# Third mixer's squares, head sums, roots and rotary exchange as fill pieces beside the second mixer's end, in a fused two-layer decode step

## The reference, cut to what matters

```python
def rope_partial(x, pos):
    ...
    x1, x2 = xr[..., :half], xr[..., half:]          # half = 8
    rot = jnp.concatenate([x1 * cos - x2 * sin, x2 * cos + x1 * sin], axis=-1)
    return jnp.concatenate([rot.astype(x.dtype), x[..., ROPE_DIM:]], axis=-1)

q_c = rope_partial(rmsnorm(q_c.reshape(B, L, H_C, D_C), lp['qn_c']), pos)
k_c = rope_partial(rmsnorm(k_c.reshape(B, L, H_C, D_C), lp['kn_c']), pos)
```

## Time and profile before

| what | value |
|---|---|
| three runs, median (lowest to highest) | 1285.93 us (1282.99 to 1288.49) |
| the profiled execution: its time, its span | 1283.79 us, 1281.9 us |
| TensorE busy (PE) | 1234.9 us, 96% of the span |
| VectorE, ScalarE, GpSimd busy | 599.8, 355.2, 134.7 us |
| mean granted TensorE clock | 0.989 of full |
| HBM | 114 GB/s over the span |
| chain that ended last | TensorE 86%, issue 4%, VectorE 4%, ScalarE 2% |

### The profile page before, as it was taken

The page is one execution under the profiler, slowest core; times in us unless marked ns, Lnnn a source line. Parts: engine busy times, 40 slices in busy tenths (PEclk is TensorE's granted clock), DMA queues, the critical chain, the costliest instruction groups (busy, mean ns, idle before and its releaser), DMA issues.

```text
span 1281.9 us, 23685 instructions
## 1 busy us (share of the span) xinstructions
PE 1234.9 (96%) x9382; PEld 920.9 (72%) x9382; DVE 599.8 (47%) x1281; ACT 355.2 (28%) x802; POOL 134.7 (11%) x204
## 2 busy tenths in 40 slices
...
GB/s 229 224 104 67 44 102 156 121 33 79 93 28 62 160 261 168 117 166 162 67 114 182 106 66 58 158 117 116 35 66 102 19 83 177 252 173 67 213 99 37
DMA packets 143368, 150.15 MB, mean 117 GB/s; under 512 B 15736, under 2 KB 130462, under 8 KB 143132
## 3 DMA queue, kind: packets, MB, share of 16 engines
...
HBM read 135.19 MB, written 11.07 MB: 114 GB/s over the span
## 4 chain that ended last, share of the span: by engine, by line
PE 86%; issue 4%; DVE 4%; ACT 2%; SPq 1%; DMA 1%; POOL 1%; ACTq 0%; DVEq 0%; POOLq 0%
PE psum L1092 57%; PE psum L1019 5%; PE psum L1253 3%; PE psum L1269 2%; PE psum L1391 1%; ACT arena L1685 1%; PE psum L1275 1%; PE psum L1134 1%; DVE arena L2192 1%; PE psum L1628 1%; PE psum L1446 1%; PE psum L1230 1%; PE psum L1458 1%; PE psum L1473 1%; PE psum L1577 1%
## 5 line engine op out<-in xcount | busy, mean ns | idle before, releaser
L1092 PE MATMUL psum<-x_b,ring 128*128 128x288 f32 x1296 | 343.1, 414 | 1.9 <-DMA ring<-in_w_in 1.1
L1092 PE MATMUL psum<-x_a,ring 128*128 128x288 f32 x1296 | 343.6, 415 | 0.5 <-DVE x_a L2145 0.4
L1092 PEld LDWEIGHTS psum<-x_b,ring 128*128 128x128 f32 x1296 | 239.9, 192 | 78.5 <-issue 17.2
L1092 PEld LDWEIGHTS psum<-x_a,ring 128*128 128x128 f32 x1296 | 240.4, 192 | 77.7 <-issue 17.0
L1685 ACT ACTIVATE arena<-psum 128x512 f32<-128x512 f32 (+9 forms) x206 | 96.9, 489 | 221.9 <-PE psum L1019 88.8
L1092 PE MATMUL psum<-z,ring 128*128 128x288 f32 x384 | 102.1, 412 | 0.0
L1092 PEld LDWEIGHTS psum<-z,ring 128*128 128x128 f32 x384 | 70.1, 190 | 20.9 <-issue 3.4
L1019 PE MATMUL psum<-consts,arena 128*128 128x128 f32 (+2 forms) x446 | 63.9, 278 | 7.6 <-DMA arena<-in_x_prompt 5.0
L1019 PEld LDWEIGHTS psum<-consts,arena 128*128 128x128 f32 (+2 forms) x446 | 50.7, 143 | 26.5 <-issue 9.8
L1092 PE MATMUL psum<-merged,ring 128*128 128x288 f32 x256 | 64.1, 414 | 3.5 <-issue 2.4
L1685 ACT ACTIVATE arena<-arena 128x256 f32<-128x256 f32 (+7 forms) x104 | 44.8, 464 | 65.8 <-DVE arena L2624 28.9
...
## 6 DMA issues: line engine op xcount, KB each, us to landing
...
```

What stands on the lines that cost most here:

```text
L1092: ins = mm(out[:, 0:NTOK], lhs, rhs(k), **flags)
```

## The change

The third mixer's preparation becomes six entries of `fillers()`: `c_sq` 0 and 1 (ScalarE's squares; with the first, GpSimd clears `CSW`; with the second, SyncE exchanges), `c_rms` 0 and 1 (head sums on TensorE into a bank of the projections, root on ScalarE) and `c_turn` 0 and 1 (VectorE's rotation). They stand between the branch projection `p_up` (0, 7) and the gate projection `p_g` (8), and wait for `b_scale` (1, 2) in place of the second mixer's end. Since `CSW` is cleared first, four transfers of 8 partitions with all 8 tiles of queries and keys replace the twelve. Their SBUF is now the arena's start. The cache's first two key pages are fetched before `b_s0` (1, 0), and clearing `CQX` moves to that place on GpSimd. `FILL` is laid out anew for the whole layer.

```diff
-PROJECTIONS = ("p_a", "p_z", "p_ba", "p_f", "p_c", "p_g", "p_up", "p_y", "p_pg", "p_ple")
+PROJECTIONS = ("p_a", "p_z", "p_ba", "p_f", "p_c", "p_g", "p_up", "p_y", "p_pg", "p_ple", "c_rms")
...
         add("b_norm6", g, 1)
+        if g == 1:
+            add("c_fetch_k", 0)
+            add("c_fetch_k", 1)
         add("b_s0", g, 0)
...
         add("b_sdec", g, 1)
-    add("c_rms", 0)
-    add("c_rms", 1)
-    for q in range(4):
-        if q < 2:
-            add("c_fetch_k", q)
-        add("c_fetch_v", q)
     add("c_rope", 0)
     add("c_rope", 1)
+    for q in range(4):
+        add("c_fetch_v", q)
     add("c_nat", 0)
...
         whole("p_up", 0, m)
+    for part in ("c_sq", "c_rms", "c_turn"):
+        for i in range(2):
+            out.append((part, i))
     for m in range(8):
...
-FILL = [0, 0, 32, 6, 0, 10, 17, 0, 19, 0, 4, 0, 6, 3, 6, 3, 18, 2, 14, 3, 0, 1, 14, 3, 0, 0, 0, 0, 0, 1, 1, 0, 0, 0,
-        0, 0, 0, 0, 0, 0, 0, 0, 0, 0, 0, 0, 1, 0, 1, 2, 3, 4, 2, 2, 2, 1, 1, 2, 5, 0, 4, 0, 0, 7, 3, 0, 0, 1, 1, 0, 1,
-        0, 0, 0, 3, 8, 5, 5, 0, 1, 7, 3, 0, 0, 12, 0, 0, 15, 0, 19, 5, 17, 8, 12, 5, 0, 0, 0, 2, 5, 0, 1, 0, 0, 2, 5,
-        0, 0, 0, 0, 0, 0, 0, 0, 0, 0, 1, 0, 0, 0, 0, 0, 0, 0, 0, 0, 0, 0, 0, 0, 0, 0, 2, 0, 2, 2, 0, 2, 0, 0, 0, 0, 9,
-        0, 0, 0, 0, 5, 0, 1, 0, 2, 0, 1, 0, 1, 1, 1, 2, 5, 3, 0, 5, 1, 1, 2, 0, 2, 1, 1, 2, 5, 3, 1, 4, 4, 1, 1, 1, 4,
-        0, 1, 0, 3, 0, 9, 0, 0, 0, 0, 0, 0, 0, 0, 0, 0, 0, 0, 0, 0, 0, 0, 0, 0, 0, 0, 0, 0, 0, 0, 0, 0, 2, 0, 4, 0, 1,
-        1, 0, 1, 0, 2, 6, 0, 0, 1, 0, 1, 0, 2, 2, 1, 0, 0, 1, 3, 2, 3, 7, 3, 0, 5, 1, 0, 6, 1, 1, 0, 4, 0, 7, 2, 2, 3,
-        6, 7, 2, 0, 7, 1, 1, 3, 1, 7, 3, 4, 4, 0, 0, 0, 21, 0, 0, 1, 3, 6, 2, 0, 0, 0, 1, 2, 5, 0, 0, 4, 1, 0, 1, 6,
-        3, 0, 4, 3, 3, 1, 2, 0, 1, 6, 4, 1, 3, 6, 3, 3]
+FILL = [0, 0, 24, 9, 8, 0, 24, 5, 12, 3, 1, 2, 5, 4, 11, 4, 11, 2, 15, 3, 1, 0, 14, 3, 0, 0, 0, 0, 0, 1, 0, 0, 0, 0,
+        0, 0, 0, 0, 1, 0, 0, 0, 0, 0, 0, 0, 2, 0, 1, 2, 2, 5, 0, 3, 0, 2, 0, 1, 5, 0, 7, 0, 3, 0, 3, 0, 1, 0, 1, 1, 0,
+        0, 0, 0, 1, 11, 2, 5, 0, 0, 0, 14, 0, 0, 14, 0, 1, 11, 0, 27, 5, 15, 7, 10, 0, 4, 2, 1, 0, 4, 0, 1, 4, 0, 0,
+        5, 0, 0, 0, 0, 0, 0, 0, 0, 0, 0, 0, 0, 0, 0, 0, 0, 0, 0, 1, 0, 0, 0, 0, 0, 0, 0, 2, 0, 3, 1, 1, 1, 0, 0, 0, 3,
+        6, 0, 1, 0, 0, 1, 3, 0, 0, 4, 0, 1, 0, 1, 1, 2, 1, 4, 3, 0, 5, 2, 2, 4, 0, 0, 0, 0, 3, 5, 4, 0, 3, 4, 1, 1, 1,
+        4, 1, 1, 0, 2, 0, 8, 0, 0, 0, 0, 0, 0, 0, 0, 0, 0, 0, 0, 0, 0, 0, 0, 0, 0, 0, 0, 0, 0, 0, 0, 0, 0, 2, 0, 2, 3,
+        1, 2, 0, 0, 0, 3, 5, 0, 1, 0, 0, 3, 0, 0, 2, 1, 0, 0, 1, 2, 2, 4, 1, 0, 4, 3, 0, 7, 1, 3, 3, 1, 1, 0, 4, 1,
+        32, 1, 3, 3, 4, 4, 0, 1, 3, 0, 2, 5, 5, 0, 0, 2, 20, 0, 1, 3, 1, 6, 2, 1, 0, 0, 2, 0, 3, 2, 0, 3, 2, 0, 0, 7,
+        3, 0, 3, 4, 3, 2, 2, 0, 0, 5, 5, 2, 3, 5, 5, 3]
...
-        CSQ = CKT[:, :, :, :].rearrange("p s a n -> p (s a n)")[:, 0:4 * NTOK].rearrange("p (a n) -> p a n", a=4)
-        CSW = CKT[:, :, :, :].rearrange("p s a n -> p (s a n)")[:, 4 * NTOK:12 * NTOK].rearrange("p (i a n) -> p i a n", i=2, a=4)
-        SQ = (CSQ, CVN[:, :, :].rearrange("p a n -> p (a n)")[:, 0:4 * NTOK].rearrange("p (a n) -> p a n", a=4))
+        SQ = arena[:, 0:8 * NTOK].rearrange("p (i a n) -> p i a n", i=2, a=4)
+        CSW = arena[:, 8 * NTOK:16 * NTOK].rearrange("p (i a n) -> p i a n", i=2, a=4)
+        CMX = part(3, 4)
+        top[0] = CQX_AT
+        CQX = part(4, NSEQ, 32)
-        CMX = part(3, 4)
-        CQX = part(4, NSEQ, 32)
+        top[0] = CKR_AT
...
+        swapped = [(h + to, h + 8 - to) for h in (0, 64) for to in (0, 8)]
...
                                           A["state_rwkv"][l, :, 4 * g + 2 * pr + hh].rearrange("s v k -> v s k")).then_inc(S.sem("rw_state_loaded"), 16)
-            def c_rms(l, i):
-                evicted(sp, "p_c", l, 4 * i + 3)
-                sp.wait_ge(S.sem("b_done"), S.count("b_done"))
-                sp.wait_ge(S.sem("b_snew"), S.count("b_snew"))
-                for to, of, n in turned:
-                    sp.dma_start(CSW[to:to + n, i, :, :], QC[of:of + n, 4 * i:4 * i + 4, :]).then_inc(S.sem(f"c_sw{i}"), 16)
+            def c_sq(l, i):
+                if i == 0:
+                    return
+                evicted(sp, "p_c", l, 7)
+                sp.wait_ge(S.sem("c_cleared"), S.count("c_cleared"))
+                for to, of in swapped:
+                    sp.dma_start(CSW[to:to + 8, :, :, :], QC[of:of + 8, 0:8, :].rearrange("p (i a) n -> p i a n", i=2)).then_inc(S.sem("c_swapped"), 16)
             def fetch(cache, l, s, dst, name):
...
                     sp.wait_ge(S.sem("b_done"), S.count("b_done"))
+                if s >= 2:
+                    sp.wait_ge(S.sem("past_k_t"), S.count("past_k_t"))
+                fetch(A["cache_k"], l, s, CKR[:, s % 2], f"past_k{s % 2}_loaded")
+            def c_fetch_v(l, s):
+                if s == 0:
                     sp.wait_ge(S.sem("b_snew"), S.count("b_snew"))
                     sp.wait_ge(S.sem("states_stored"), S.count("states_stored"))
-                if s >= 2:
-                    sp.wait_ge(S.sem("past_k_t"), S.count("past_k_t"))
-                fetch(A["cache_k"], l, s, CKR[:, s % 2], f"past_k{s % 2}_loaded")
-            def c_fetch_v(l, s):
                 if s >= 4:
...
             def c_rms(l, i):
-                pe.wait_ge(S.sem("squares"), S.count("squares"))
+                n = proj_no[S.at]
+                pe.wait_ge(S.sem("squares"), S.count("squares", pos[("c_sq", l, i)]))
+                pe.wait_ge(S.sem(freed()), S.count(freed(), proj_at[n - 3]))
+                for h in range(4):
+                    ins = mm(bank()[32 * h:32 * h + 32, 0:NTOK], C("sum_head"), SQ[:, i, h, :], start=True, stop=True)
+                ins.then_inc(S.sem("projected"), 1)
+            def c_rope(l, i):
                 pe.wait_ge(S.sem("b_snew"), S.count("b_snew"))
-                sum4(i, SQ[i], C("sum_head"))
-            def c_rope(l, i):
-                pe.wait_ge(S.sem("inv_roots"), S.count("inv_roots", pos[("c_rms", l, 1)]))
+                pe.wait_ge(S.sem("inv_roots"), S.count("inv_roots", pos[("c_rms", l, i)]))
                 pe.wait_ge(S.sem("c_rope"), S.count("c_rope", S.at - 1))
-                spread4(SQ[i][:, 0, :], C("spread_head"), 32)
+                spread4(SQ[:, i, 0, :], C("spread_head"), 32)
             def c_nat(l, i):
...
                 act.wait_ge(S.sem("out_roots"), S.count("out_roots"))
+            def c_sq(l, i):
+                evicted(act, "p_c", l, 4 * i + 3)
+                act.wait_ge(S.sem("b_scaled"), S.count("b_scaled", pos[("b_scale", l, 1, 2)]))
+                fn(SQ[:, i, :, :], QC[:, 4 * i:4 * i + 4, :], ACT.Square).then_inc(S.sem("squares"), 1)
+                act.wait_ge(S.sem("squares"), S.count("squares"))
             def c_rms(l, i):
-                evicted(act, "p_c", l, NC3 - 1)
-                act.wait_ge(S.sem("b_done"), S.count("b_done"))
-                act.wait_ge(S.sem("b_snew"), S.count("b_snew"))
-                fn(SQ[i][:, :, :], QC[:, 4 * i:4 * i + 4, :], ACT.Square).then_inc(S.sem("squares"), 1)
-                act.wait_ge(S.sem("squares"), S.count("squares"))
-                act.wait_ge(S.sem("square_sums"), S.count("square_sums"))
-                inv_root(SQ[i][:, 0, :], M[i][:, 0:NTOK], 1.0 / 64, "c_eps").then_inc(S.sem("inv_roots"), 1)
+                act.wait_ge(S.sem("projected"), S.count("projected"))
+                fn(SQ[:, i, 0, :], bank()[:, 0:NTOK], ACT.Ln, bias=C("c_eps"), scale=1.0 / 64).then_inc(S.sem(freed()), 1)
+                act.wait_ge(S.sem(freed()), S.count(freed()))
+                fn(SQ[:, i, 0, :], SQ[:, i, 0, :], ACT.Exp, scale=-0.5).then_inc(S.sem("inv_roots"), 1)
                 act.wait_ge(S.sem("inv_roots"), S.count("inv_roots"))
             def c_nat(l, i):
...
+                act.wait_ge(S.sem("states_stored"), S.count("states_stored"))
...
-            def c_rms(l, i):
-                dve.wait_ge(S.sem(f"c_sw{i}"), S.count(f"c_sw{i}"))
+            def c_turn(l, i):
+                dve.wait_ge(S.sem("c_swapped"), S.count("c_swapped"))
...
                           "states_stored")
-            def c_nat(l, i):
+            def c_sq(l, i):
                 if i == 0:
+                    pool.wait_ge(S.sem("b_scaled"), S.count("b_scaled", pos[("b_scale", l, 1, 2)]))
+                    pool.memset(CSW[:, :, :, :], 0.0).then_inc(S.sem("c_cleared"), 1)
+                    pool.wait_ge(S.sem("c_cleared"), S.count("c_cleared"))
+            def c_fetch_k(l, s):
+                if s == 0:
+                    pool.wait_ge(S.sem("b_done"), S.count("b_done"))
+                    link(pool.memset(CQX[:, :, :, :], 0.0))
+            def c_rope(l, i):
+                if i == 0:
                     pool.wait_ge(S.sem("c_rope"), S.count("c_rope"))
-                    pool.wait_ge(S.sem("b_snew"), S.count("b_snew"))
```

(29 more changed lines are left out.)

6 lines of the change are left out of this document (3 added, 3 removed).

## The result

The changed kernel takes 1276.82 us (median of 15 runs, 1273.32 to 1279.46) against 1282.99 us of the kernel before in the same session (15 runs, 1277.82 to 1291.55): ratio 0.9942, interval 0.9924 to 0.996. The forecast was 1275.3 us, 10.6 us less than 1285.93, within 1268 to 1287, and faster by more than 0.5%. The time lies in the range, 1.5 us over the forecast; it is faster by 0.58%, and the interval (0.40 to 0.76%) reaches under 0.5%. The measured gain, 6.2 us by the medians, is less than the 10.6. The profiled executions took 1283.79 and 1277.75 us.

A forecast was written before the change was run, and what follows sets the result against it. It took TensorE's work, its waits and its lower clock to bound the kernel. Terms +0.4 - 2.9 - 4.2 - 1.0 - 6.8 + 1.9 + 0.6 + 1.4 = -10.6 us off 1285.93 gave 1275.3 us, range 1268 to 1287.

The forecast's parts named there:

- The move itself: Third mixer's preparation in its new place: stays hidden but for a 0.2 us wait at `b_norm5`, +0.4 us for both layers.
- rival 2: At `b_norm5`: the exchange lands late, TensorE waits 3.8 us, with lower clock behind it; 1289.3 us, chance 0.09.
- `a_sout`: TensorE's wait ahead of `a_sout`: three more pieces cover 1.45 of 1.80 us, -2.9 us for two layers.
- `b_lora`: TensorE's wait of 2.09 us ahead of `b_lora`: five more pieces cover it, -4.2 us.
- `a_u`: TensorE's wait ahead of `a_u` (2): 11 pieces become 12, -0.5 of 0.75 us each, -1.0 us.
- `a_spread` and `a_convout`: Ahead of `a_spread` 0 and `a_convout`: one piece fewer at each, a payment of +1.9 us.
- `b_kk`: Between `b_lora` 0 and `b_kk`: 22 pieces become 20, a payment of 0 to +1.9 us, taken +0.6.
- `c_sout` (1) to `p_up` 2: Behind `c_sout` (1): 3 pieces become 1, so TensorE waits 0.7 us, a payment of +1.4 us.
- The clock: Half-clock stretches behind three long waits at `a_sout` and `b_lora` go, -6.8 us, bounds 0 and -6.8.
- Rival 1: TensorE's clock: the lower level comes at other places instead; sum -3.8, 1282.1 us, chance 0.18.
- Rival 3: Places pieces are taken from: waits of the same size come up there instead; 1286 us, chance 0.13.
- rival 4: The preparation's new place gives nothing and all gain is `FILL`'s; no time of its own, no chance given.

The follow-up runs named there:

- e9: The kernel before with the new `FILL` up to `a_norm5` (2) alone, its own behind it: 1281.7 us, ratio 0.9968.
- e3: The kernel before with four more pieces ahead of `b_lora` 0 alone, taken from between there and `b_scale` (0, 0): 1281.0 us, ratio 0.9982.
- e11: The kernel before with the next layer's parameter loads put behind the last `p_up` instead of ahead of it: 1281.4 us, ratio 0.9971.
- e2: The kernel before with the new `FILL` up to `b_scale` (0, 0), its own behind it, third mixer not moved: 1274.8 us, ratio 0.9944.
- e5: The changed kernel with pieces moved to places where it waits, as many as before ahead of `b_hist`: 1272.8 us, ratio 0.9894.
- e6: The kernel before with the new `FILL` up to `b_scale` (0, 0), pieces in it moved to where TensorE waited, third mixer not moved: 1272.0 us, ratio 0.9891.

## Why the prediction was right, and where it was off

**The move itself: sizes right, its end slightly over.** Memset 2.04 us (2.1 forecast), fourth issue from 434.98 (435.0), release at 438.94 (438.8), rotation over at 447.25 (447.2), `b_norm5`'s product at 447.70 (447.6), TensorE there at 447.37 (447.5). Differences of 0.1 us on both sides made 0.48 us out of 0.2: +1.0 in place of +0.4 us. The landing scattered by more than that, from 2.8 to 4.0 us after the end of the last issue over the fourteen times that the seven kernels with the new place made it. One argument against rival 2 was wrong: each of the four transfers has the 8 partitions of those that did the exchange before, with twice the tiles, and not an eighth of the partitions.

**`a_sout`: -2.1 in place of -2.9.** Three more pieces should have covered 1.45 of 1.80 us and covered 1.06. The chain did behave as forecast: from the start of `a_sout` 0 to the end of VectorE's last layout it took 10.71 us before (183.97 to 194.68) and 10.72 after (187.20 to 197.92). The term that was mis-sized is the price of a piece. Timeline before (the rest is in the earlier trace rows), then of the changed kernel:

```profile
183.97 1.13 PE L1340 MATMUL psum<-arena 32*128 32x512 f32 x4
...
185.02 0.75 PE L1092 MATMUL psum<-x_b,ring 128*128 128x288 f32 x2
```

```profile
187.20 1.99 PE L1349 MATMUL psum<-arena 32*128 32x512 f32 x8
...
189.12 7.06 PE L1101 MATMUL psum<-x_b,ring 128*128 128x288 f32 x28
...
194.94 2.98 DVE L2390 TENSOR_TENSOR arena<-arena,consts 64x512 f32<-64x512 f32 x1
```

The lone piece between `a_sout` 0 and 1 was taken away. With it TensorE needed 2.79 us up to the first piece behind `a_sout` 1 (183.97 to 186.76), without it 1.92: the piece had held 0.87 us, not 0.485. The four more pieces in the long row are 1.94; 1.94 - 0.87 = 1.07 us.

**`b_lora`: -3.5 in place of -4.2.** I had counted five pieces from `a_norm5` (2). The runs show four. The chain starts where ScalarE reads the last piece of a `p_z` tile (204.77 us before): from there to `b_lora` it takes 17.14 us before, 17.14 in e9, 17.13 in e3 and 17.31 in the changed kernel. That piece has a fixed place in the list, so what counts is how many pieces of the list stand ahead of `b_lora`, 279 before and 283 after. 4 x 0.485 = 1.94 of the 2.09 us; e9 and e3 bear it out, and in the changed kernel 0.32 us are left.

**`a_u`** gave 1.0 us as forecast. **`a_spread` and `a_convout`** cost 1.3 - 0.3 and 0.9 us, together 1.9: as forecast. **`b_kk`** paid nothing (0.6 forecast); no wait over 0.2 us came up there. The waits at `a_l2` fell by 0.5 us in the two layers together, which was in no term.

**`c_sout` (1) to `p_up` 2: the wait right, its price half.** 0.60 and 0.59 us for 0.7 forecast. In layer 0 it cost nothing, because `p_y` behind it had waited for SyncE anyway (2.43 us, now 1.09). The step took a wait for its price without asking who waits next. The fall of that `p_y` wait, and the 3.41 us at 0.50 behind it, were in no term; in return a key page in layer 1 waits 0.94 us, where before one waited 0.40 and another 0.30, and the wait of 0.5 us at L2681 behind it is new; these weren't in one either.

**The clock: about -4 in place of -6.8; that -5.6 came out is partly luck.** The -6.8 was the price of the three stretches of the earlier trace rows, and of these one is left, at half its length. But the -5.6 holds the stretch at the first `p_y` as well, which was in no term and is worth some 2 us (e11: -1.7). Three kernels have the new `FILL` of the first mixer and still wait 1.99 to 3.10 us at that `p_y`: e2, e5 and e6. Their clock losses are 9.1, 7.9 and 9.1, so 3.5 to 4.8 under 12.6 (2.6 to 5.1 under before of their own sessions, each to 1 or more). The step that was mis-sized is taking all three stretches of one profile at their full length: the means give back a little over half. Nor do e3 (+0.9) and e9 (-1.3 for up to -5.1) give it back one wait at a time, though their profiles have lost the stretches. Why the means fall short of the profiles isn't shown. Rival 1, in which none of the term comes, falls by e2, e5 and e6; some of it was true. The Trainium skill ("TensorE: Matmul & The Clock Gate", "Part 1: The HAM clock gate") lets the number of slow matmuls at a kernel's start vary run by run. The start-up products above agree with it, 1.87 or 3.46 us for the same sixteen. Behind the waits of 1.80 us at `a_sout` such luck doesn't show: both layers of all four profiles have the stretch.

**The sum.** Without the clock I had -3.8 us and the means show -3.3; with it -10.6 and -8.9. Both agree better than their terms do: too much at `a_sout`, `b_lora` and the three stretches, too little at `b_norm5`, and the gain at `p_y` that I didn't see. The rest of the distance to the session's -6.2 I put down to the scatter of both kernels between sessions and to the start, which the runs don't show: before had medians of 1282.99, 1283.37, 1285.26 and 1285.94, the changed kernel 1276.82 and 1274.03. Rival 3 (waits only wander) falls by the second experiment, and rival 4 was right: the gain is `FILL`'s.
